# Mixer projections and output product of a two-layer hybrid kernel: from f32 matmuls to three float32r products of split halves

## The reference, cut to what matters

```python
proj = h @ w_in                                  # 1024 x 3584
qa, ka, va, qd, kd, vd, qh, fh, ih, gh = split(proj)
o_a = stick_breaking(qa, ka, va)                 # 4 heads of 64, cumulated log weights
o_d = dilated_mixture(rope(rmsnorm(qd)), rope(rmsnorm(kd)), vd)   # 4 heads of 64
o_h = rmsnorm(hgrn2(silu(qh), 1 - exp(log_f(fh)), ih, log_f(fh))) * silu(gh)   # 4 heads of 128
y = concatenate([o_a, o_d, o_h]) @ w_out         # 1024 x 1024
x = x + g2 * y
```

## Time and profile before

| | |
|---|---|
| three runs | 1746.22, 1746.29, 1747.24 us |
| profiled execution, its own time | 1745.78 us |
| its span | 1743.7 us |
| mean granted TensorE clock | 0.952 of 2.4 GHz |
| busy: PE, DVE, ACT, POOL | 1574.5, 979.8, 602.9, 203.9 us |
| the two mixers, residual to residual | 178.5 us each |

### The profile page before, as it was taken

One profiled execution on the slowest core, in us unless ns is written; L12 is line 12 of the kernel. 1 busy time (PEld: TensorE's weight loads), 2 busy tenths in 40 slices (PEclk: granted clock), 3 DMA queues, 4 the chain that ended last, 5 costly groups with the idle time before them and its releaser, 6 DMA issues.

```text
span 1743.7 us, 21727 instructions
## 1 busy us (share of the span) xinstructions
PE 1574.5 (90%) x8944; PEld 1237.1 (71%) x8944; DVE 979.8 (56%) x1482; ACT 602.9 (35%) x944; POOL 203.9 (12%) x205
## 2 busy tenths in 40 slices
PE   6978759899788998999998998989999999989998
PEld 1635536645648997786548997779987875579986
DVE  0257585767527777445336777667774453354444
ACT  2214311142115443353125443244433541244442
POOL 0020341100000110014000110001100251001100
PEclk9999969998699999999998999989999999989999
DMA  9324224236245888432345886838876222355651
GB/s 343 114 96 148 94 73 146 73 139 260 97 157 193 267 281 305 150 121 73 98 138 168 284 290 247 320 127 285 283 288 213 97 97 97 97 160 178 194 170 48
DMA packets 192105, 305.44 MB, mean 175 GB/s; under 512 B 6139, under 2 KB 116487, under 8 KB 191879
## 3 DMA queue, kind: packets, MB, share of 16 engines
q1 hardware_dynamic: 189088, 299.45, 50.7%
q10 hardware_dynamic: 2919, 4.61, 0.7%
HBM read 302.99 MB, written 1.05 MB: 174 GB/s over the span
## 4 chain that ended last, share of the span: by engine, by line
PE 73%; DVE 10%; issue 6%; ACT 6%; DMA 2%; POOL 2%; ACTq 0%; DVEq 0%; POOLq 0%
PE ps L373 71%; DVE accs L514 2%; PE ps L376 1%; DVE wlo L1940 1%; ACT whi L1898 1%; DMA ring<-in_w_mod_dram 1%; DMA ring<-in_ffn_w_down_dram 1%; DVE arena L1197 1%; DVE arena L1194 1%; DVE H L1787 1%; DVE H L1721 1%; ACT arena L1432 0%; DVE misc L1499 0%; POOL misc L1768 0%; ACT hhi L1903 0%
## 5 line engine op out<-in xcount | busy, mean ns | idle before, releaser
L1940 DVE TENSOR_TENSOR wlo<-ring,whi 128x1024 fp32r<-128x1024 f32 x264 | 322.7, 1225 | 235.4 <-ACT whi L1898 230.0
L373 PE MATMUL ps<-hhi,whi 128*128 128x256 f32 x1408 | 407.4, 289 | 22.9 <-DVE hlo L1946 16.7
L373 PE MATMUL ps<-hlo,whi 128*128 128x256 f32 x1408 | 403.8, 287 | 0.0
L373 PE MATMUL ps<-hhi,wlo 128*128 128x256 f32 x1408 | 403.7, 287 | 0.0
L1898 ACT ACTIVATE whi<-ring 128x1024 fp32r<-128x1024 f32 x264 | 275.2, 1055 | 309.5 <-PE ps L373 277.5
L373 PEld LDWEIGHTS ps<-hhi,whi 128*128 128x128 f32 x1408 | 275.8, 196 | 24.9 <-DVE hlo L1946 23.7
L373 PEld LDWEIGHTS ps<-hlo,whi 128*128 128x128 f32 x1408 | 275.7, 196 | 1.2 <-issue 1.2
L373 PE MATMUL ps<-ring,H 128*128 128x512 f32 (+1 forms) x608 | 266.2, 589 | 11.0 <-ACT arena L2075 5.5
L373 PEld LDWEIGHTS ps<-hhi,wlo 128*128 128x128 f32 x1408 | 275.5, 196 | 0.0
L373 PEld LDWEIGHTS ps<-ring,H 128*128 128x128 f32 x608 | 115.1, 196 | 131.2 <-issue 115.8
L514 DVE SCALAR_TENSOR_TENSOR accs<-ring,misc,accs 128x512 f32<-128x512 f32 x266 | 201.1, 756 | 3.0
(11 more groups left out here) (288 smaller groups left out, 1402.6 us busy)
## 6 DMA issues: line engine op xcount, KB each, us to landing
ring<-in_w_mod_dram SPq DMA_DIRECT2D x84, 1024.0 KB, 7.3
ring<-in_w_in_dram SPq DMA_DIRECT2D x48, 1024.0 KB, 5.1
ring<-in_ffn_w_gate_dram SPq DMA_DIRECT2D x44, 1024.0 KB, 6.8
ring<-in_ffn_w_up_dram SPq DMA_DIRECT2D x44, 1024.0 KB, 5.4
ring<-in_ffn_w_down_dram SPq DMA_DIRECT2D x44, 1024.0 KB, 6.6
ring<-in_w_out_dram SPq DMA_DIRECT2D x12, 1024.0 KB, 4.8
gates<-in_b_mod_dram SPq DMA_DIRECT2D x7, 512.0 KB, 6.4
ring<-in_w_proj_a_dram SPq DMA_DIRECT2D x2, 1024.0 KB, 5.9
```

What stands on the lines that cost most here:

```text
L373: return self.e.matmul(o, lhsT, rhs, start=start, stop=stop)
L1940: v.done(v.e.tensor_tensor(lo, M.slot(key)[:, r0:r0 + rn, :], plain(hi), ALU.subtract), ("split", l, sub, n), *([M.freed(key)] if ends els ...
```

## The change

In the mixers every projection and the output product become three float32r products (`mm3`). The tokens are split into `MHI` and `MLO`. The weights are split in 36 pieces n = 0 to 35 of 128x1024: one for each of the 28 steps, eight for the output product. ScalarE writes the high half of piece n into one of four buffers (`act_high`, which waits until TensorE is through with piece n-4), VectorE or GpSimd writes the low half over the weights in the ring (`low_weights`). Pieces in `ON_POOL` go to GpSimd, the others to VectorE. In `in_steps` ScalarE's step n now begins with the high half of piece n+3, VectorE's ends with the low half of piece n+3, if that is its own. GpSimd has its pieces at fixed places of its program: 0 and 1 before the join, 2, 3, 5, 7 and 9 before the levels of the recurrence, the others after them. `Y`'s transposes are split too (`YHI` on ScalarE, `YLO` by a new `v_turned` on VectorE). The buffers are shared with the gate rows, the `accs` tile and others, so the loads of the second layer's gate biases wait for the first mixer's residual. `act_join`'s scratch moves to `JS`.

```diff
-        self.ring = self.sb("ring", [128, NS, 2048])
+        self.ring, self.ring_r = self.twice("ring", [128, NS, 2048])
...
-        self.gates = self.sb("gates", [128, 4, 1024])
-        self.accs = self.sb("accs", [128, 2, 512])
-        self.H = self.sb("H", [128, 8, 512])
+        self.gates, self.gates_r = self.twice("gates", [128, 4, 1024])
+        self.accs, self.accs_r = self.twice("accs", [128, 2, 512])
+        self.H, self.H_r = self.twice("H", [128, 8, 512])
...
+    def twice(self, name, shape):
+
+        with self.nc.sbuf_tensor(name, shape, f32) as plain_:
+            pass
+        return plain_, self.sbr(f"{name}_r", shape)
...
+    def slot_r(self, key):
+        n, a, b = self.slots[key]
+        return self.ring_r[:, n % NS, 0:a * b].rearrange("p (a b) -> p a b", b=b)
...
+        self.at = 23552
+        self.JS = take(2, 1024)
+        kt = lambda a: a.rearrange("p (k t) -> p k t", t=256)
+        ahi = self.AHI[:, :, :].rearrange("p k t -> p (k t)")
+        self.MHI, self.MLO = kt(self.TAIL[:, 0:2048]), self.H_r[:, :, 256:512]
+        self.YHI = kt(self.WHI[:, 2:4, :].rearrange("p a b -> p (a b)"))
+        self.YLO, self.DX0_r, self.GH_r = kt(ahi[:, 1536:3584]), ahi[:, 3584:4608], self.WLO[:, 1, :]
...
-    ends = {2: ("residual", "first"), 5: ("residual", 0, 0), 8: ("residual", 0, 1)}
+    ends = {2: ("residual", 0, 1), 5: ("residual", 0, 1), 8: ("residual", 0, 1)}
     free = {5: ("fence", "delta"), 8: ("fence", "delta")}
     for key, parts in (("first", [(0, p) for p in range(5)]), ((0, 0), [(0, p) for p in range(5, 9)]),
                        ((0, 2), [(1, p) for p in range(5)]), ((1, 0), [(1, p) for p in range(5, 9)])):
...
         for hf in range(2):
-            a.wait_ge(("x", l, sub, blk, hf), ("modps", chunks_before(M, l, sub)), ("ss", l, sub, blk - 1))
-            a.done(a.e.activation(M.accs[:, hf, :], M.X[:, blk, hf * 512:hf * 512 + 512], ACT.Square,
+            a.wait_ge(("x", l, sub, blk, hf), ("ss", l, sub, blk - 1))
+            a.done(a.e.activation(M.JS[:, 0, hf * 512:hf * 512 + 512], M.X[:, blk, hf * 512:hf * 512 + 512], ACT.Square,
                                   accum_out=M.ss4[:, 2 * blk + hf:2 * blk + hf + 1]), ("ss", l, sub, blk))
 
 
...
+
+def weights(M, l, n):
+
+
+    j = n % 2
+    if n < 12:
+        key, at = ("wf", l, FEATS[n // 4][0], n % 4 // 2), (slice(0, 8), slice(j * 128, j * 128 + 128))
+    elif n < 28:
+        key, at = (("tok", l, TOKS[n // 4 - 3][1]), "w", n % 4 // 2), (slice(2 * j, 2 * j + 2), slice(0, 512))
+    else:
+        key, at = ("out", ("x", l), 2 * OUTS[(n - 28) // 2]), (slice(j, j + 1), slice(0, 1024))
+    return key, M.slot(key)[:, at[0], at[1]], M.slot_r(key)[:, at[0], at[1]], j == 1
+
+
+def split_weights(M, l, n):
+
+
+    key, w, lo, ends = weights(M, l, n)
+    g = ((0, 1), (3, 0))[l]
+    t = (M.gates_r[:, g[0], :], M.accs_r[:, :, :].rearrange("p a b -> p (a b)"), M.gates_r[:, g[1], :], M.GH_r if n < 28 else M.DX0_r)[n % 4]
+    return key, t.rearrange("p (a b) -> p a b", b=w.shape[2]), lo, ends
+
+
+def act_high(a, l, n):
+    M = a.M
+    if n == 0:
+        a.wait_ge(("residual", "first") if l == 0 else ("residual", 0, 2))
+    elif n == 1:
+        a.wait_ge(("modps", chunks_before(M, l, 1)))
+    elif n == 2:
+        a.wait_ge(*[("gated", l, 1, 1, hf) for hf in range(2)])
+    elif n == 3:
+        a.wait_ge(("d", l, 0, 1))
+    elif n == 31:
+        a.wait_ge(("lq", l, 6))
+    key, w, _, _ = weights(M, l, n)
+    a.wait_ge(key, ("staged", l, 1, n - 4))
+    a.done(a.e.activation(split_weights(M, l, n)[1], w, ACT.Copy), ("whi", l, 1, n))
+
+
+def low_weights(lane, l, n):
+    M = lane.M
+    _, hi, lo, _ = split_weights(M, l, n)
+    lane.wait_ge(("whi", l, 1, n))
+    lane.done(lane.e.tensor_tensor(lo, weights(M, l, n)[1], plain(hi), ALU.subtract), ("split", l, 1, n))
+
+
+def act_highs(a, l):
+    for n in range(3, 31):
+        act_high(a, l, n)
+        yield
+
+
+def v_lows(v, l):
+    for n in range(3, 31):
+        if n not in ON_POOL:
+            low_weights(v, l, n)
+        yield
+
+
+def in_steps(lane, l, proj, rec, stick, dil, first, ahead, behind):
 
     proj, rec, stick, dil = proj(lane, l), rec(lane, l), stick(lane, l), dil(lane, l)
     for step in range(28):
+        tick(ahead)
         if first:
             tick(proj)
         if step >= 4:
@@ -2032,6 +2118,7 @@
             tick(dil)
         if not first:
             tick(proj)
+        tick(behind)
     run(proj, rec, stick, dil)
 
 
@@ -2042,19 +2129,32 @@
 
 
 def pe_projections(pe, l):
-    M = pe.M
+    M, n = pe.M, 0
     for name, _, flag in FEATS:
         for j in range(4):
-            key = ("wf", l, name, j // 2)
             b = pe.bank(("f", l, name, j), "proj")
-            pe.wait_ge(key)
+            key, hi, lo, ends = split_weights(M, l, n)
+            pe.wait_ge(("split", l, 1, n))
             for kt in range(8):
-                pe.wait_ge(*[("h", l, 1, blk, kt // 4) for blk in range(2)])
-                ins = pe.mm(b[:, 0:256], M.slot(key)[:, kt, (j % 2) * 128:(j % 2) * 128 + 128], M.H[:, kt, 0:256], kt == 0, kt == 7)
-            pe.done(ins, ("f", l, name, j), *([M.freed(key)] if j % 2 else []))
+                pe.wait_ge(("hlo", l, 1, kt // 4))
+                ins = pe.mm3(b[:, 0:256], (hi[:, kt, :], lo[:, kt, :]), (M.MHI[:, kt, :], M.MLO[:, kt, :]), kt == 0, kt == 7)
+            pe.done(ins, ("f", l, name, j), ("staged", l, 1, n), *([M.freed(key)] if ends else []))
+            n += 1
             yield
     for _, name in TOKS:
-        yield from pe_tok(pe, ("tok", l, name), 0, "proj")
+        out = ("tok", l, name)
+        bs = [pe.bank((out, blk), "proj") for blk in range(2)]
+        for q in range(4):
+            key, hi, lo, ends = split_weights(M, l, n)
+            pe.wait_ge(("split", l, 1, n))
+            for i in range(2):
+                kt = 2 * q + i
+                for blk in range(2):
+                    c = slice(blk * 128, blk * 128 + 128)
+                    ins = pe.mm3(bs[blk], (M.MHI[:, kt, c], M.MLO[:, kt, c]), (hi[:, i, :], lo[:, i, :]), kt == 0, kt == 7)
+            pe.done(ins, ("staged", l, 1, n), *([M.freed(key)] if ends else []), *([(out,)] if q == 3 else []))
+            n += 1
+            yield
 
 
 def act_projections(a, l):
...
+    for n in (2, 3, 5, 7, 9):
+        low_weights(g, l, n)
     for t in M.KL:
         g.done(g.e.memset(flat(t), 0.0), ("zero", l))
     for lv in range(3):
...
             pool_rstd(g, ("q", l), 8)
+    low_weights(g, l, 21)
     pool_rstd(g, ("k", l), 8)
+    for n in (23, 25, 27):
+        low_weights(g, l, n)
     pool_rstd(g, ("y", l), 8)
+    for n in (29, 31, 33, 35):
+        low_weights(g, l, n)
 
 
 
...
+    a.done(a.e.activation(M.YHI[:, 2 * kp:2 * kp + 2, :], M.ps(key).rearrange("p (k t) -> p k t", k=2), ACT.Copy), ("yhi", l, kp))
+
+
+def v_turned(v, l, kp):
+    M, key = v.M, ("turn", l, kp)
+    v.wait_ge(("yhi", l, kp))
+    v.done(v.e.tensor_tensor(M.YLO[:, 2 * kp:2 * kp + 2, :], M.ps(key).rearrange("p (k t) -> p k t", k=2),
+                             plain(M.YHI[:, 2 * kp:2 * kp + 2, :]), ALU.subtract), ("free", key), ("yt", l, kp))
 
 
 def act_stick(a, l):
...
+    yield
+    v_turned(v, l, 0)
     yield
 
 
...
-    in_steps(pe, l, pe_projections, pe_recurrence, pe_stick, pe_dilated, True)
+    in_steps(pe, l, pe_projections, pe_recurrence, pe_stick, pe_dilated, True, iter(()), iter(()))
     bs = [[pe.bank(("o", name, blk, hf), "outx") for hf in range(2)] for blk in range(2)]
 
     def product(*kps):
         for blk, kp, k in [(b, kp, k) for b in range(2) for kp in kps for k in range(2)]:
-            key, n = ("out", name, 2 * kp), OUTS.index(kp)
-            pe.wait_ge(key, ("yt", l, kp))
+            at = OUTS.index(kp)
+            n, c = 28 + 2 * at + k, slice(blk * 128, (blk + 1) * 128)
+            key, hi, lo, ends = split_weights(M, l, n)
+            pe.wait_ge(("split", l, 1, n), ("yt", l, kp))
             for hf in range(2):
-                ins = pe.mm(bs[blk][hf], M.YT[:, 2 * kp + k, blk * 128:(blk + 1) * 128], M.slot(key)[:, k, hf * 512:hf * 512 + 512],
-                            n == 0 and k == 0, n == 3 and k == 1)
-            if k == 1:
-                pe.done(ins, *([("o", name, blk)] if n == 3 else []), *([M.freed(key)] if blk else []))
+                s = slice(hf * 512, hf * 512 + 512)
+                ins = pe.mm3(bs[blk][hf], (M.YHI[:, 2 * kp + k, c], M.YLO[:, 2 * kp + k, c]), (hi[:, 0, s], lo[:, 0, s]),
+                             n == 28, n == 35)
+            if blk or n == 35:
+                pe.done(ins, *([("o", name, blk)] if n == 35 else []), *([("staged", l, 1, n)] if blk else []),
+                        *([M.freed(key)] if blk and ends else []))
 
     product(0)
     pe_dilated_end(pe, l)
@@ -2572,26 +2693,57 @@
 
 
 def act_mixer(a, l):
-    for blk in range(2):
-        act_modulated(a, l, 1, blk)
```

(61 more changed lines are left out.)

## The result

The changed kernel takes 1759.2 us (median; 1756.87 to 1762.18) against 1746.26 us in the same session: a ratio of 1.0075, 95% interval 1.0058 to 1.0093, so 12.9 us slower. The prediction was 1757.0, range 1725 to 1773, with "slower" the likeliest. The profiled execution has a span of 1756.5 us at a mean granted clock of 0.936.

A forecast was written before the change was run, and what follows sets the result against it. TensorE, 90% busy, was to save 24.2 us a mixer, but splits delay the recurrence and masking chains: 12.0 us late to the fourth tail, less 6.5, so 5.5 a mixer, 11.0 in all: 1757 us, range 1725 to 1773.

The forecast's parts named there:

- Start: Mixer start to FH copy: first product +2.8 us, slow clock +2.7, cheaper steps give back 2.3; FH copy 3.1 late.
- To step 10: FH copy to step 10: splits delay scan, level 0 and the bank; step 10 starts at +26.2 us, 3.1 more.
- a rival with 14%: GpSimd needs 3.0 us per low half and TensorE loses its clock at step 10: +4 and +4 per mixer, 1773; 14%.
- Steps 10 to 12: Three steps save about 1.9 us, the QKA copy behind level 3 takes 1.3 back: -0.6 us.
- Scores to tail: Stick scores to fourth tail product: high 16, lows 17 and 18, a late start and turns add 6.4 us.
- The rest: Fourth tail to mixer end: cheaper products save 14.3 us; slow clock, K path and `yg` take some back; sum -6.5.
- The slow stretch behind the K path: After the dilated heads' K path: a second stretch of slow TensorE clock, costing 1.7 us.
- the K path: Dilated heads: behind `v_turned` and GpSimd's lows 23 and 25, about 3.8 us late at its transposes.
- One sign: Sign of being right, whole kernel: TensorE's busy time some 45 us lower and the span not.
- neither sign of being wrong: Level 0 on GpSimd starting less than 3 us after the scan, or tails within 22 us of the stick scores.
- The chains have room: Both mixers: without mutual hindrance at the lows, level 0 and K path in time, about 9 us faster each, 1728; 22%.
- Cancel: Whole kernel: lateness and savings cancel, 1743 to 1750, with the forecast's mechanisms at two thirds of their size; 14%.

The follow-up runs named there:

- e4: The changed kernel plus four float32 products of 512 columns that nothing reads, in TensorE's gap at the start; 1.0044 of the kernel before.
- e2: The changed kernel with pieces 0 to 11 left float32 and tokens split only behind both halves of their modulation; 0.9960 of the kernel before.
- e3: The changed kernel with pieces 0 to 19 left float32 and tokens split only behind both halves of their modulation; 0.9932 of the kernel before.
- e1: The changed kernel with only the first four high halves made, standing in for all others and every low half (output wrong); 1710.2 us, 0.9806 of the kernel before.
- e9: The changed kernel with pieces 0 to 15 left float32, 16 to 35 split and every low half on VectorE; 0.9888 of the kernel before.
- e5: The changed kernel with every low half from piece 3 on moved to VectorE; 1.0010 of the kernel before.
- e11: The changed kernel with low halves from piece 3 on moved to VectorE, plus four unread float32 products before each mixer's first product; 1.0002 of the kernel before.
- e12: The changed kernel with low halves of pieces 21 to 35 moved to VectorE, 3, 5, 7 and 9 staying on GpSimd; 1.0021 of the kernel before.

## Why the prediction was right, and where its terms were off

The direction, the size and most of the mechanism held: 12.9 us by the medians, 13.6 in the two profiled mixers, against a forecast of 11.0. Two terms missed in opposite directions, and that they cancelled was luck. By its own steps, the first mixer first:

1. **Start.** First product 12.2 us after the residual (forecast 12.0), then slow records, then the FH copy 26.2 us after it instead of 23.35: 2.9 late, forecast 3.1. In the second mixer it is 1.6 late (24.9 against 23.3): the granted clock is 0.68 over the first 5.3 us there, and 0.50 in the first mixer. e4 shows the clock as a part of its own, e2 and e3 that the rest goes with the feature split and its split tokens.
2. **To step 10.** Step 10 starts 27.8 us after the FH copy (785.84 - 758.07), not 26.2: 4.7 more than before, where 3.1 was forecast. The steps between are right: the scan is 1.8 late beyond the copy's own lateness (forecast 1.9), the low half and the memsets hold level 0 for 3.9 behind it (forecast 3.9), level 0 is through 24.4 after the copy (24.6), and the bank of step 10 is free after 26.0 (26.2). But TensorE isn't there yet, so there is no wait at step 10 either. What I left out is that steps 7 and 9 wait, for VectorE's QH copies, and that TensorE then runs slowly: the granted clock is 0.61 from 769.67 to 774.00 and 0.60 from 779.70 to 784.00. I had weighed a lost clock for step 10 alone (a rival with 14%); it was 1.00 there. e1 has the same two waits, so the cheaper products bring them about and the splits lengthen them; its clock stays at 1.00 behind both. In the second mixer only the wait at step 7 cost the clock (0.50 against 1.00 behind step 9's 1.26 us), and step 10 starts 26.1 after the copy, 3.0 more than before.
3. **Steps 10 to 12.** Not -0.6 but +0.7: the diagonal mask's bank is late as well (wait of 2.28 us at 791.20). The scores are 8.2 late, forecast 5.6. In the second mixer this step is +6.1 and the scores are 10.7 late: the wait is 3.79 us, and behind it the clock falls, which it doesn't in the first. From that wait to the last copy of the scores, both mixers:
```profile
791.20:804.75 13.55, 13.55 (x101) 12.59 (x101) 12.28 (x12) 5.48 (x10) 8.60 (x5) 1.00 0.23 77
1416.78:1434.24 17.46, 17.46 (x101) 16.49 (x102) 10.84 (x12) 5.40 (x11) 9.75 (x5) 0.76 0.19 61
```
4. **Scores to tail.** 24.6 us from the copy's start, forecast 27.4, before 20.9. The +6.4 was +3.7, in both mixers, and e9 measures 3.6 for the halves with their turns. I had added a late start; there was none. Terms 2 and 3 are too small by 2.9 and term 4 too large by 2.7: the tail is 11.9 late in the first mixer and 14.3 in the second, forecast 12.0. That the sum up to here hit in the first mixer is luck. The wait at the tail was 4.26 and 3.35 us, not 6.
5. **The rest.** -4.4 and -8.2 us, mean -6.3, forecast -6.5. The two mixers differ here by the clock alone. The same 88 records behind a wait of 1.60 us, in both:
```profile
866.15:884.84 18.69, 18.69 (x88) 15.18 (x88) 8.75 (x10) 6.68 (x21) 6.41 (x3) 0.83 0.23 79
1494.69:1510.53 15.84, 15.84 (x88) 12.96 (x88) 8.75 (x10) 6.57 (x21) 6.43 (x3) 1.00 0.27 94
```
That is 2.9 us, and right behind the tail another 0.9 (clock 0.87 and 0.92 over the next 21 us). The slow stretch behind the K path that I put at 1.7 is the first of these; the second mixer doesn't have it, and no run shows what decides. e1 gives the saving without splits as 13.0 (forecast 14.3), e5 with all late splits off GpSimd as 12.0. So where the clock up to the output product is alike, GpSimd's late low halves cost 3.8 us a mixer (84.7 against 80.9 from the tail to the end): 1.2 up to the 1.60 us wait, the K path, which I had 3.8 late at its transposes (their wait was 1.01 us, 863.89); 1.9 from there to the output product, whose wait of 3.62 us comes by the softmax chain, which I had not followed; 0.7 in the output product, whose 144 records run at 0.94 behind that wait and at 1.00 in e5.

The low half on GpSimd takes 2.39 us (mean of the four whose high half lies in `gates_r`; most others take 2.37 to 2.49, and the longest, 3.26, lies beside VectorE's rotation), not 2.0. One sign was misread in advance: TensorE's busy time was to fall by some 45 us and fell by 24, against 49.0 in e1. The difference of 25 us goes with the slow clock, at which the records last longer (0.21 against 0.12 us apart); the mean clock is 0.936, and 0.953 in e1. Of the other signs, the 0.21 us records and the longer VectorE subtractions came, the wait at step 10 didn't, and neither sign of being wrong showed. "The chains have room" (22%) is refuted at its own turning point, since level 0's input came 4.7 and 3.2 us later, not under 3. "Cancel" (14%) is what e5 and e11 show once GpSimd's late halves are gone. The rule of the Trainium skill that I used (page "SBUF — State Buffer", section "Who interferes with whom") is borne out by the rows: a VectorE `tensor_tensor` with both inputs in SBUF takes 3.13 instead of 1.23 us beside a GpSimd one, while `tensor_reduce` (one input) has a mean of 954 ns in the change and 954 in e5, and one that lies wholly inside a low half on GpSimd takes its usual 1.22:
```profile
889.34 2.83 POOL L2090 TENSOR_TENSOR ring_r<-ring,ahi 128x1024 fp32r<-128x1024 f32 x1 [6.48 <-ACT ahi L2083]
889.97 1.22 DVE L2659 TENSOR_REDUCE misc<-arena 128x4 f32<-128x1024 f32 x1
```
What I took from the rule, 5 us over both mixers, was too small: the late halves alone cost 7.6 by point 5, and e5 and e12 shorten the two profiled mixers by 10.4 and 12.0. No run separates the hold from the rest that goes with GpSimd, such as its 2.39 us for a low half against 1.23 on VectorE.

## What to carry to other kernels

Before a cheaper product is bought with extra elementwise work, split the span by what TensorE waits for: here the saving arrived at 13 of 14 us where TensorE set the pace, and at 3 of 10 where a recurrence did (e1), and there the extra operations only made that chain longer. An extra operation costs by its place in a queue, not by its length: one that waits for a late producer delays all behind it, on whichever engine it stands. And a spare engine that stops another one's operations isn't spare: giving 8 low halves a mixer back from GpSimd to the busier VectorE was worth 9 us of this kernel by the medians (e12), 12 in the profiled mixers. Last, one profile is one draw of the clock: two mixers of the same kernel differ by 3.8 us behind the tail for no other reason.

## What the runs showed of the hardware

- TensorE's clock fell at more places than the start: after waits of 3.16, 2.57 and 4.26 us the granted clock was 0.61, 0.60 and 0.50 in the next 4 us; in the kernel before it was 0.69 over the 5.4 us behind the wait of 2.40 us, which I had not looked at. After the 2.57 us wait three records still come at the full rate (779.91, 780.03, 780.14) before they spread to 0.21 us apart. The length of the wait doesn't settle it: behind 1.60 us the clock was 0.50 in the first mixer and 1.00 in the second, and behind 2.53 us in e1 it was 1.00.
- A VectorE operation beside a GpSimd one with SBUF inputs is stopped rather than slowed: the subtraction of 880.82 ends 1.09 us after GpSimd's low half, near its own 1.23. The 128x256 product of the rotation (L2635) has a mean of 1518 ns in the change, and 418 in e5.
- GpSimd's own operations are held too: `pool_level`, 1.89 us at its shortest before, takes 2.81 at 786.58, and its mean went from 2104 ns to 2386.
